# First two tiles behind three norms from x without its root; maxima and query decays spread by DMA

## The reference

```python
def rmsnorm(x, g):
    return x * rsqrt(mean(x * x, -1) + EPS) * g
def modulate(x, g, shift, scale):
    return rmsnorm(x, g) * (1 + scale) + shift
# for each layer i
hn = modulate(x, norm_g[i, 0], mod[0], mod[1])
x = x + mod[2] * mixer(hn)
hn = modulate(x, norm_g[i, 1], mod[3], mod[4])
x = x + mod[5] * (square(relu(hn @ mlp_w_up[i])) @ mlp_w_down[i])
# in the mLSTM, for one head: b running sum of log forget gates, m running maximum
s = (q @ k.T) * exp(dmat - m)
num = s @ v + exp(inter - m) * (q @ C0)
h = num / max(abs(den), exp(-m))
```

## Time and profile before

| | |
|---|---|
| Median of 3 runs | 1409.12 us (1404.42 to 1409.48) |
| Profiled execution, its own time | 1405.48 us |
| Its span | 1403.7 us |
| Instructions | 26248 |
| PE busy | 1337.7 us (95%) |
| DVE busy | 674.6 us (48%) |
| POOL busy | 525.4 us (37%) |
| ACT busy | 344.0 us (25%) |
| Mean granted clock of TensorE | 0.98 |

### The profile page before, as it was taken

How to read it: one execution, slowest core, us unless ns; L and a number is a source line. 1 busy time by engine, 2 the same in 40 slices (tenths; PEclk the granted TensorE clock), 3 DMA queues, 4 the chain that set the end, 5 groups by cost and what they waited for, 6 DMA issues and landing times.

```text
span 1403.7 us, 26248 instructions
## 1 busy us (share of the span) xinstructions
PE 1337.7 (95%) x11609; PEld 1296.0 (92%) x11609; DVE 674.6 (48%) x1043; ACT 344.0 (25%) x530; POOL 525.4 (37%) x248
## 2 busy tenths in 40 slices
PE   5899999897999999999999799999799999999997
PEld 4798889897999999999999799999799999999996
DVE  2714435655641441431437507858772461541774
ACT  3532442211321221221222322112221221221221
POOL 1433424342333433334335244435243344443440
PEclk9999999998999999999999899999899999999998
DMA  9665113654346545455443132323133323333221
GB/s 330 217 151 127 33 29 113 203 160 153 120 136 186 154 143 179 142 161 167 148 139 91 37 100 87 89 84 91 40 96 91 89 78 92 90 91 91 78 73 64
DMA packets 237970, 166.41 MB, mean 119 GB/s; under 512 B 5419, under 2 KB 210967, under 8 KB 237730
## 3 DMA queue, kind: packets, MB, share of 16 engines
q1 hardware_dynamic: 215946, 121.33, 29.5%
q10 hardware_dynamic: 21752, 43.35, 9.8%
q0 software_dynamic: 160, 0.07, 0.0%
HBM read 157.82 MB, written 6.91 MB: 117 GB/s over the span
## 4 chain that ended last, share of the span: by engine, by line
PE 87%; DVE 6%; issue 3%; DMA 2%; ACT 2%; POOL 0%; SPq 0%; POOLq 0%; DVEq 0%; ACTq 0%
PE G L1364 59%; PE G L1386 18%; PE B L1405 3%; PE B L1350 1%; DVE small_s L1308 1%; DVE yc L1307 1%; DMA xin<-in_x_sample 1%; PE B L1601 1%; DMA raw<-in_mlstm_w_out 1%; PE B L1568 1%; PE B L1603 1%; PE B L1441 1%; ACT wh L446 1%; PE B L1586 1%; PE B L1673 1%
## 5 line engine op out<-in xcount | busy, mean ns | idle before, releaser
L717 POOL TENSOR_TENSOR wl<-raw,wh 128x1024 fp32r<-128x1024 f32 x192 | 484.5, 2526 | 717.7 <-ACT wh L446 717.7
L446 ACT ACTIVATE wh<-raw 128x1024 fp32r<-128x1024 f32 x192 | 203.1, 1058 | 501.9 <-PE G L1364 208.9
L1364 PE MATMUL G<-Xh,wh 128*128 128x272 f32 x1440 | 306.6, 294 | 1.0 <-POOL wl L717 1.0
L1364 PE MATMUL G<-Xl,wh 128*128 128x272 f32 x1440 | 297.9, 288 | 0.0
L1364 PE MATMUL G<-Xh,wl 128*128 128x272 f32 x1440 | 296.5, 287 | 0.0
L1364 PEld LDWEIGHTS G<-Xh,wh 128*128 128x128 f32 x1440 | 224.4, 189 | 14.1 <-issue 11.9
L1364 PEld LDWEIGHTS G<-Xl,wh 128*128 128x128 f32 x1440 | 226.6, 189 | 0.0
L1364 PEld LDWEIGHTS G<-Xh,wl 128*128 128x128 f32 x1440 | 225.8, 189 | 0.0
L1364 PE MATMUL G<-Hh,wh 128*128 128x272 f32 x864 | 180.5, 290 | 0.0
L1364 PE MATMUL G<-Hl,wh 128*128 128x272 f32 x864 | 178.8, 288 | 0.0
L1364 PE MATMUL G<-Hh,wl 128*128 128x272 f32 x864 | 177.7, 287 | 0.0
(11 more groups left out here) (299 smaller groups left out, 1509.7 us busy)
## 6 DMA issues: line engine op xcount, KB each, us to landing
aring<-in_ada_w ACTq DMA_DIRECT2D x78, 512.0 KB, 4.8
raw<-in_mlp_w_up SPq DMA_DIRECT2D x64, 512.0 KB, 4.1
raw<-in_mlp_w_down SPq DMA_DIRECT2D x64, 512.0 KB, 3.8
raw<-in_mlstm_w_in SPq DMA_DIRECT2D x24, 512.0 KB, 4.2
raw<-in_conv_w_in SPq DMA_DIRECT2D x24, 512.0 KB, 3.7
early<-in_ada_w SPq DMA_DIRECT2D x16, 512.0 KB, 12.3
raw<-in_mlstm_w_out SPq DMA_DIRECT2D x8, 512.0 KB, 5.2
raw<-in_conv_w_out SPq DMA_DIRECT2D x8, 512.0 KB, 3.7
```

The costliest lines, as they stand in the source:

```text
L446: nc.scalar.activation(wh[:, t % SLOTS], raw[:, t % RAWS], ACT.Copy).then_inc(s_hi, 1)
L717: nc.gpsimd.tensor_tensor(wl[:, t % SLOTS], raw[:, t % RAWS], wh[:, t % SLOTS].bitcast(F32), ALU.subtract).then_inc(s_lo, 1)
L1364: last = mm(G[:, 2 * (g % 2) + hf, 0:HALF], w[:, s, k, :], x[:, k, hf * HALF:(hf + 1) * HALF], start=st, stop=en)
```

## The change

Three things are done.

*The first two tiles behind norms 1, 2 and 3.* The root belongs to a token, a column, so it can be multiplied on after the product. The new operand `XP` holds x times gain without the root (`raw_hi` on ACT, `raw_lo` and `raw_samples` on DVE), made tile by tile beside the residuals, and six further columns in the two halves for the shifts (278 columns instead of 272). PE runs the first pair of tiles on it (`first_pair`), with `stats` behind step (2,1) and `spread` behind step (4,1). DVE then multiplies the result by the root and adds the shift's product for the samples (`scale_first`); ACT adds that of the prompt as a bias. The second pair (`second_pair`) and all later tiles take the normed x as before. The root is copied to `xr` in SBUF. On ACT the high parts of tiles t0+3, t0+4 and t0+5 now stand before and between the norm's steps.

*Maxima and query decays.* L1560 and L1579 are gone. The rows go to DRAM once and come back, repeated over the partitions, by DMAs on ACT's queue: `row_spread` one a head, `query_decays` two every second head. The exponential and the scaling work in place in SBUF. `scaled_queries` stands behind `weights`.

*Order.* SP fetches the third weight tile of the output projection before x comes back from DRAM. In the output projection the modulation matmuls stand behind tiles 1, 3, 4, 5 (before 1, 3, 5, 6), and two of the modulation vectors change places.

```diff
+XH = HALF + SB // 2 + 2
+FIRST_STATS, FIRST_SPREAD = (2, 1), (4, 1)
+ADA_AFTER_W = {1: 0, 3: 1, 4: 2, 5: 3}
+ADA_ORDER = (0, 1, 2, 4, 3, *range(5, 2 * NMOD))
...
-            unit(T_WOUT, w_out, 0, order=range(2))
+            unit(T_WOUT, w_out, 0, order=range(3))
             sp.wait_ge(s_ys, 1)
...
+            def raw_hi(n, k):
+                act.wait_ge(s_gn, n + 1)
+                act.wait_ge(s_dr, (0, G_WOUT, G_MLP0_LAST + 8, G_COUT)[n] + k + 1)
+                nc.scalar.activation(prompt(XP[n][0][:, k, :]), prompt(xT[:, k, :]), ACT.Identity, scale=gain[:, k, 0:1])\
+                    .then_inc(s_xph, 1)
+
+            def first_unit(n, t0, g0, layer, which, finish, evac, after={}, ada=None):
+                raw_hi(n, KT - 1)
+                hi(t0 + LEAD)
+                norm_hi(n, layer, which, (0, 1))
+                finish(n, 0, g0)
+                norm_hi(n, layer, which, (2,))
+                finish(n, 1, g0 + 1)
+                norm_hi(n, layer, which, (3,))
+                if 1 in after:
+                    after[1]()
+                if ada is not None:
+                    ada_next(4 * ada + ADA_AFTER[1])
+                hi(t0 + LEAD + 1)
+                norm_hi(n, layer, which, (4,))
+                hi(t0 + LEAD + 2)
+                norm_hi(n, layer, which, (5, 6, 7))
...
+            def row_spread(h):
+                if h >= 2:
+                    act.wait_ge(s_pv, h - 1)
+                else:
+                    act.wait_ge(s_nm, 16)
+                    act.wait_ge(s_spill, 16)
+                nc.scalar.dma_start(dexp[h % 2][:, :], negm[h:h + 1, :].broadcast_to((P, SEQ))).then_inc(s_row[h % 2], 16)
...
+            def query_decays(a):
+                if a:
+                    act.wait_ge(s_pv, 2 * a)
+                else:
+                    act.wait_ge(s_em, 16)
+                    act.wait_ge(s_kx, X_NORM0 + KT)
+                for h2 in range(2):
+                    h = 2 * a + h2
+                    nc.scalar.dma_start(qt[DK * h2:DK * (h2 + 1), :], edec[h:h + 1, :].broadcast_to((DK, SEQ - P))).then_inc(s_qin, 16)
...
+            lo(T_CG + LEAD)
+            pool.wait_ge(s_used, T_CG + 2)
             nc.gpsimd.memset(u[:, :, 0:2], 0.0).then_inc(s_cre, 1)
-            lows(T_CG + LEAD, T_MLP1 + LEAD)
+            lows(T_CG + LEAD + 1, T_MLP1 + LEAD)
...
+            def raw_lo(n, k):
+                dve.wait_ge(s_xph, KT * (n - 1) + k + 1)
+                V.scalar_tensor_tensor(prompt(XP[n][1][:, k, :]), prompt(xT[:, k, :]), gain[:, k, 0:1],
+                                       prompt(XP[n][0][:, k, :].bitcast(F32)), ALU.mult, ALU.subtract)\
+                    .then_inc(s_xp, 1)
+
+            def raw_step(n, m, layer, which):
+                if m == KT - 3:
+                    raw_shifts(n, layer, which)
+                if m == KT - 2:
+                    raw_samples(n, 0, KT - 1)
+                if m == KT - 1:
+                    raw_samples(n, KT - 1, KT)
+                for k in {0: (), KT - 2: (KT - 3, KT - 2), KT - 1: (KT - 1,)}.get(m, (m - 1,)):
+                    raw_lo(n, k)
+
+            def scale_first(n, o, t0, g0):
+                g = g0 + o
+                dve.wait_ge(s_used, t0 + o + 1)
+                ps = G[:, 2 * (g % 2):2 * (g % 2) + 2, :]
+                s = stage[g % 2][:, :]
+                V.tensor_copy(bcol[:, o:o + 1], ps[:, 0, XH - 1:XH])
+                chain.link(V.tensor_tensor(halves(s), ps[:, :, 0:HALF], halves(xr[:, :]), ALU.mult))
+                V.tensor_tensor(sample4(s), sample4(s),
+                                ps[:, :, HALF:HALF + SB // 2].unsqueeze(3).broadcast_to((P, 2, SB // 2, ST)), ALU.add).then_inc(s_sc, 1)
...
+                chain.link(V.tensor_copy(halves(xr[:, :]), rstd))
...
                     V.scalar_tensor_tensor(prompt(hb[k % 2][:, :]), prompt(xT[:, k, :]), gain[:, k, 0:1],
-                                           rstd[:, :, 0:PH], ALU.mult, ALU.mult).then_inc(s_hh, 1)
+                                           prompt(xr[:, :]), ALU.mult, ALU.mult).then_inc(s_hh, 1)
...
+            LAGGING = ((0, 0), (1, 0), (0, 1), (1, 1), *IN_STEP[4:])
...
+            def first_pair(n, t, g):
+                def norm_steps(k, o):
+                    if (k, o) == FIRST_STATS:
+                        stats(n)
+                    if (k, o) == FIRST_SPREAD:
+                        spread(n)
+                def raw_ready(k):
+                    pe.wait_ge(s_xp, KT * (n - 1) + k + 1)
+                    if k in (0, KT - 1):
+                        pe.wait_ge(s_xps, 2 * (n - 1) + (1 if k == 0 else 2))
+                pair_steps(t, g, XP[n][0], XP[n][1], XH, IN_STEP, slots_drained(g), raw_ready, norm_steps)
+
+            def second_pair(n, t, g, ready):
+                pair_steps(t, g, XN[n][0], XN[n][1], HALF, LAGGING, lambda o: pe.wait_ge(s_sc, 2 * (n - 1) + o + 1), ready)
...
-                        mm(B4[:, :], sel2[:, h, :], negM2[:, :], start=True, stop=True).then_inc(s_bc, 1)
...
-                        if h % 2 == 0:
-                            last = mm(B6[:, 0:SEQ - P], selp[:, a, :], erow[:, :], start=True, stop=True)
```

More of the change, by code:

```diff
@@ L483, in ada_next @@
                     ada_fetch(nc.scalar, a)
-            def unit(t0, g0, evac, j=None, per_t=0, per_g=0):
+            def raw_hi(n, k):
[19 more added lines that the diff above has]
+                norm_hi(n, layer, which, (5, 6, 7))
+                for m in range(2, KT):
+                    if m > 2:
+                        hi(t0 + m + LEAD)
+                    evac(t0 + m, g0 + m, None, 0, 0)
+                    if ada is not None and m in ADA_AFTER:
+                        ada_next(4 * ada + ADA_AFTER[m])
@@ L589, in maxima_out, with rows_out @@
                                         sample4(rows[0][:, :])[:, hf, :, ST - 1]).then_inc(s_bo, 16)
[L591 to L592 removed]
+            def rows_out():
+                nc.scalar.dma_start(negm.rearrange("h (a c) -> h a c", a=2), prompt(rows[4][:, :])).then_inc(s_nm, 16)
+            def row_spread(h):
                 if h >= 2:
@@ L1279, in _ @@
             combine(11)
-            unit(G_MLP0_LAST + 8, residual(5, 2))
-            norm_apply(2, 1, 0)
+            norm_gain(2, 1, 0)
+            down_residual = residual(5, 2)
+            for m in range(KT):
+                down_residual(m, G_MLP0_LAST + 8 + m, None, 0)
+                raw_step(2, m, 1, 0)
+            norm_apply(2, 1, 0, T_CG, G_CG)
             for m in range(KT):
@@ L1314, in _ @@
             unit(G_BG, drain_square(Hh, Hl, yc))
-            unit(G_COUT, residual(NMOD + 2, 3))
-            norm_apply(3, 1, 1)
+            norm_gain(3, 1, 1)
+            conv_residual = residual(NMOD + 2, 3)
+            for m in range(KT):
+                conv_residual(m, G_COUT + m, None, 0)
+                raw_step(3, m, 1, 1)
+            norm_apply(3, 1, 1, T_MLP1, G_MLP1)
             for q in range(QUARTERS - 1):
@@ L1369, in tile, with pair_steps @@
                         between(k)
-            def tile_pair(t, g, xh, xl, j, per_t, per_g, ready):
-                ahead = 5
-                for k, o in (*((k, o) for k in range(ahead) for o in range(2)),
-                             *((k, o) for o in range(2) for k in range(ahead, KT))):
+            PAIR_AHEAD = 5
+            IN_STEP = (*((k, o) for k in range(PAIR_AHEAD) for o in range(2)),
+                       *((k, o) for o in range(2) for k in range(PAIR_AHEAD, KT)))
+            LAGGING = ((0, 0), (1, 0), (0, 1), (1, 1), *IN_STEP[4:])
+            def pair_steps(t, g, xh, xl, width, order, free, ready, between=None):
+                for k, o in order:
                     if k == 0:
-                        split_wait(pe, t + o, j, per_t)
-                        if g + o >= 2:
-                            pe.wait_ge(s_ev, at(g + o - 1, j, per_g))
+                        split_wait(pe, t + o, None, 0)
+                        free(o)
                     if o == 0:
@@ L1389, in tile_pair, with slots_drained, free, first_unit @@
                         last.then_inc(s_used, 1)
+                    if between is not None:
+                        between(k, o)
+            def slots_drained(g):
+                def free(o):
+                    if g + o >= 2:
+                        pe.wait_ge(s_ev, g + o - 1)
+                return free
+            def tile_pair(t, g, xh, xl, j, per_t, per_g, ready):
+                pair_steps(t, g, xh, xl, HALF, IN_STEP, slots_drained(g), ready)
+            def first_pair(n, t, g):
[11 more added lines that the diff above has]
+                pair_steps(t, g, XN[n][0], XN[n][1], HALF, LAGGING, lambda o: pe.wait_ge(s_sc, 2 * (n - 1) + o + 1), ready)
+            def first_unit(n, t0, g0, ready, ada=None, between=None, behind=None):
+                first_pair(n, t0, g0)
+                if behind is not None:
+                    behind()
+                if ada is not None:
```

(13 more changed lines are left out.)

242 lines of the change are left out of this document (145 added, 97 removed).

## The result

The changed kernel took 1397.68 us in the median of five runs (1396.19 to 1400.14), against 1409.06 us before: a ratio of 0.9927, 95% interval 0.9909 to 0.9944, so 0.7% faster. A second comparison gave 0.9923 (0.9908 to 0.9938). The forecast was 1392, the range 1372 to 1403, and "faster by over 0.5%" had 0.83. The number held, in part by luck. The terms behind it did not: the value stage, which was to give 5.3 us, gave 1.4 in one execution and lost 3.0 in another, and the smallest edit, the fetch order, gave most.

What follows compares the result with a forecast made beforehand. TensorE, 87% of the span, was taken to bound the kernel: 5.9 (norms) - 2.0 (clock) + 5.3 (value stage) + 1.3 (queries and keys) + 3.7 (output projection) = 14.2 us off 1405.48, forecast 1392, range 1372 to 1403.

Steps and rivals of the forecast that it cites:

- The norms: Norms 1 to 3: tile 4 starts earlier, gaining 2.9, 1.5 and 1.5 us, 5.9 in sum.
- (a): Norm 2, first pair's start: DVE reaches the last residual 2.0 us late; PE goes on at 3.0, losing 2.2 us.
- (c): Norm 2, after the spread: DVE copies the root and scales; PE starts the second pair at 19.6 us, costing little.
- (d): Norm 2, second pair: DVE sets the pace, two POOL splits hold it 4.5 us; tile 4 starts at 37.9 us.
- (b): Norm 2, first pair: POOL's split holds `diag` until 11.5 us, PE loses 1.6; the first pair's steps end at 18.4.
- The clock at the norms: Norms: only the gap of about 4.5 us might bring 1.2 GHz; charged at one of three norms, 2.0 us.
- The value stage: V stage: two products leave PE, shortening odd heads by 0.6 us, even by 0.75; 5.3 us taken, bounds 3 and 8.5.
- The output projection: Before the output projection: earlier fetch of the third weight tile removes PE's 3.66 us gap; gain 3.7, bound 3.0.
- A: Norms and V stage: POOL's splits fall between DVE's instructions; 1378 us, or 1364 to 1370; chance 0.30.
- B: Norms: the clock falls in the first pair as well, 3.0 us there; no measurable change, 1405 us; chance 0.12.
- C: V stage: query decays land late by DMA, near 14 us; slower, 1416 us; chance 0.05.
- D: Behind the norms: loss moves to tiles 4 and 5, split late, 2 us a norm; 1398 us; 0.53 together with the forecast.

Runs made afterwards that it cites:

- pair_alone: Kernel before the change, with only the first pair behind norms 1 to 3 on x without its root: ratio 0.9986, 2.0 us by the ratio.
- e3: Changed kernel, with POOL's split of tile t0+3 moved ahead of the power of norms 1 to 3: 1394.64 us, ratio 0.9896.
- e2: Changed kernel, with ACT's high parts of tiles t0+4 and t0+5 moved behind the norm's eight steps: 1392.93 us, ratio 0.9882.
- e8: Changed kernel, with the scaling `hb` reading the root from PSUM instead of the SBUF copy `xr`: 1390.20 us, ratio 0.9868.
- e4: Changed kernel, with POOL's split in each value-stage head moved from behind the mask to behind the chunk states: 1389.92 us, ratio 0.9862.
- e1: Kernel before the change, with only the output projection's third weight tile fetched before x comes back: 1402.28 us, ratio 0.9949.

## Why the prediction was right, and where it was not

- **The norms.** Forecast 5.9 less 2.0 for the clock; measured 3.3 and 4.0 in the two profiles, and 2.0 by the ratio of pair_alone. Steps (a) to (c) came within 0.5 us at norm 1: second step at 2.5, `diag` held for 3.00 us, end of the first pair at 18.4, second pair at 19.5. The two holds in (d) came as computed, with 4.1 us for 4.5, and the eighth k was ready at 33.8 for 34.9 (norm 1). The holds decided, as weighed in (b) and (d): e3, e2 and e8 each take an instruction away from a split, or let it read PSUM, and shorten exactly that instruction. The rule of the Trainium skill, page "SBUF — State Buffer", section "Who interferes with whom", on two SBUF inputs is what e8 shows: beside a split `hb` took 0.75 us with one, and `Xl` and `Yl` 2.1 to 2.3 with two.
- **The clock at the norms** was mis-sized. I charged 2.0 in all, as one fall in three. In the two profiles the falls behind the stand cost 1.6 + 1.8 and 0.8 + 1.7 + 0.8 us (against 7.05 at full clock), and the first pair of norm 2 another 1.5 (5.62 and 5.64 us for 4.12 behind its step at 1.2 us of waiting): some 5 us. The argument that failed here is that only a gap longer than 3.66 us could cost clock: 1.20 us did, and 3.87 did where 3.66 had not.
- **The value stage is the step that failed.** "So an odd head's loop is 12.62 - 0.15 - 0.5 = 12.0" and "12.75 for 13.5" in even heads. Measured in order from the second head on: 12.1, 13.4, 12.6, 15.2, 11.8, 13.3. In the odd head with the masks on POOL nothing was gained, since its loop already ended 0.15 us before PE did; the prediction read this and still counted 0.6 for it. In even heads I took the loop from the time of before, in which the split lay in the shadow of a wait for PE; taking PE's product away uncovered it. I had priced DVE's hold from the earlier trace rows and did not ask whether it would newly occur here. Gain 1.4 and -3.0 for a forecast of 5.3; without the hold 9.0 (e4). The difference between the two profiles is the low clock behind the stands of the fifth and the seventh head.
- **The output projection.** 3.7 forecast, 3.0 and 6.3 in the stretch, 7.0 by medians (e1). The mechanism was right; its size was read from an execution in which the stand cost no clock.
- **Queries and keys** gave 1.4 to 1.6 for 1.3.
- **The sum.** By the ratios of the parts alone, the norms gave 2.0 for 3.9, value stage with queries and keys 0.7 for 6.6, the projection 7.2 for 3.7: 9.9 for 14.2, each with an interval of some 2 us to either side. So a miss of 5.9 and one of 1.9 were partly paid by a surplus of 3.5 that was not foreseen; that is the luck in the number. The forecast of 1392 lies 17.1 under the median of 1409.06, the measured median 11.4. Of this 5.7, 2.8 are the sum, and 2.9 come from setting it against an execution 3.6 us under the median. What that execution lacked is in the main the low clock behind the stand that the change removes (2.5 of the 4.7 us to the second profile).
- Rivals: A (the port does not bind) is refuted by `diag` at 3.00 us and the two of 2.8. B named a clock falling in the first pair, and one of the signs of being wrong, a granted clock under 0.9 there, did come at norm 2 (0.75 for 6.7 us), but it cost 1.5 us and not 3. C did not come: the row DMAs landed in 3.7 and 2.8 us (medians) for the 4 that were charged, and no wait of DVE is on a DMA. Its arithmetic was off as well: with a landing near 14 us the 8 us beyond 6 at three heads are already 24, and the spread rows would have come on top. D (tiles 4 and 5 split late) did not show in the changed kernel; in e2 the loss moved to tile 4, but it waited for its bank.

## What to carry to other kernels

When work is taken from the engine that sets the time, look at what ran in the shadow of the waits for it: another engine's instruction that was free there may now hit the loop, and the gain becomes a hold. Place GpSimd's large splits where VectorE is idle, or let the VectorE instruction of two tensors beside them read one from PSUM; a cast with one input in SBUF was held all the same (e3). Price a stand of TensorE as its length plus what the clock may take behind it, and read that from more than one execution.

## What the runs showed of the hardware that was not expected

- Stands of nearly the same length left different clocks: 3.66 us with 1.00 behind it and 3.87 us with 0.63; 3.5 us with 0.68 and 1.00 in one execution.
- Short stands are not safe: the 1.55 us in the fifth head had a granted clock of 0.53 behind it (179 to 182 us). The 12 matmuls there took 2.94 to 3.02 us in five of six profiled executions with this stand, and 1.70 in the sixth (e3). Behind 1.20 us in the first pair of norm 2 it was 0.75.
- Where one operand lies decides a hold of 2.05 us: beside the start of the same split, the scaling `hb` took 2.80 us with the root in SBUF and 0.75 with it in PSUM. A cast of 128x32 elements, with one input in SBUF, took 2.37 for 0.18.
